# Twelve pipelined units in the preparation of the recurrence, and the condition vectors loaded first

## The chip, the cores and the metric

The kernel runs on one core of a Trainium2 chip, in one launch. The metric is the device time of that launch in microseconds (us), as a median of runs. The core has five engines, each with an instruction queue of its own: TensorE (PE) multiplies matrices and writes to PSUM, VectorE (DVE), ScalarE (ACT) and GpSimd (POOL) work element by element, and SyncE (SP) here only issues DMA transfers between DRAM and SBUF. Queues run in order and meet through semaphores.

## The reference

Two transformer blocks follow one another on 1024 tokens of width 1024. The change touches the first block's token mixing, and there the RWKV branch (8 heads of 64), and the conditioning vectors ahead of it. Cut to what matters (`rw` is the convolved part of `h @ w_in` for the 1024 latent tokens, `rwc` that for the 256 context tokens):

```python
rw = depthwise_conv(u[..., RET_COLS:], conv_w)          # width 3, along the tokens

def rwkv_prepare(u, w0, w2, a0, a2, g2, k_k, k_a, r_k):
    r, k, v, wl_f, wl_b, al, gl_f, gl_b = split_cols(u, RWKV_SPLITS)
    def decay(wl, w0_d, w2_d):
        w_log = -jax.nn.softplus(-(w0_d + jnp.tanh(wl) @ w2_d)) - 0.5
        return heads(jnp.exp(-jnp.exp(w_log)))
    iclr = jax.nn.sigmoid(a0 + al @ a2)
    kk = heads(k * k_k)
    kk = kk / jnp.maximum(jnp.linalg.norm(kk, axis=-1, keepdims=True), 1e-12)
    k_mod = heads(k * (1.0 + (iclr - 1.0) * k_a))
    bonus = (jnp.sum(r * k_mod * r_k, axis=-1, keepdims=True) * v)
    g_f, g_b = jax.nn.sigmoid(gl_f) @ g2[0], jax.nn.sigmoid(gl_b) @ g2[1]
    return (r, decay(wl_f, ...), decay(wl_b, ...), k_mod, v, -kk, kk * heads(iclr), g_f, g_b, bonus)
# the recurrence then runs forward and backward over these, in chunks of 64 tokens
```

At the very start, `silu(c) @ w_mod + b_mod` and `silu(c_ctx) @ w_mod + b_mod` give shifts, scales and gates (`w_mod` is 1024 x 6144, 25.2 MB in f32).

## The kernel before

The program is a chain of stages. A stage (`Stage`) allocates its tiles and semaphores, runs blocks in which each engine has its own code, and ends with a meeting of all engines and the clearing of its semaphores; the next stage starts after that. Nothing of a stage overlaps the next. The stages around the change are, in order: a block that loads two tables (`cst`, `col`); `modulation` (tiles `mod_*`); the norms and projection (`norm_*`, `proj_*`, which writes `uT`, the projected channels as rows over 1280 tokens); `retention` (`ret_*`); `rwkv_prepare` (`prep_*`); `rwkv_chunks` (`chunks_*`), which turns each of 40 blocks of 128 tokens by 128 channels into small matrices; `rwkv_states` (`states_*`), which runs the recurrence over 20 chunks from them; `rwkv_combine` (`comb_*`).

`modulation`: SP streams `w_mod` as 24 transfers of 1 MB through a ring of six buffers; a buffer is taken again when PE has used it. PE cannot begin before ACT has applied silu to the two vectors. ACT issues the two vector loads with one value (4 bytes) a descriptor, then 40 small loads of bias and gains, and only then waits for the vectors and applies silu.

`rwkv_prepare` has two blocks. The first convolves the four low-rank inputs on DVE. The second loops over `PAIRS` = 4 pairs of heads (128 channels, all `TT` = 1280 tokens at once). For one pair, DVE convolves r, k and v (L784 to L788, five instructions each), makes running sums of the decay rates (L980 to L986), normalises `kk` (L992 to L994, with a reciprocal of 1280 columns), and multiplies results out; POOL makes four of the eight results (L900). ACT applies Sigmoid, Square, Sqrt and Exp. The eight results of a pair go to DRAM (`prim`) through four buffers `prep_out`; v goes to `vT`; gates and bonus to `gate` and `bonus`. SP also stores the decay at each chunk's end, one value of 4 bytes at a time, to `wc` (L865), ahead of the eight stores of `prim` (L871) in its queue. All of a pair's products, stores and vector work use the same single buffers, and the next pair starts when DVE has seen all of it done (L1013 to L1015).

`rwkv_chunks` loads for each block `prim` (L1069), `vT` (L1070) and `wc` (L1072); PE waits for all three. `rwkv_states` loads all of `wc` (L1480) ahead of `re` in SP's queue (16 transfers, tile `states_r`), and ACT's queue loads `yi` beside it; DVE's first step waits for `wc`, PE's fourth for the first eight transfers of `re`.

## Time and profile before

| | before |
|---|---|
| median of 3 runs | 5389.64 us (5381.85 to 5392.05) |
| the profiled execution, its own time | 5381.96 us |
| its span, first to last instruction | 5379.8 us |
| mean granted clock of TensorE | 0.886 of full speed (2.4 GHz) |
| PE busy | 4132.7 us, 77% of the span |
| DVE busy | 2557.6 us, 48% |
| ACT busy | 1687.2 us, 31% |
| POOL busy | 409.5 us, 8% |
| DRAM traffic | 844.30 MB, mean 157 GB/s |

These shares are means over stages that have different limits. Since stages don't overlap, each is to be read by itself: its length, and what its engines wait for. On this core a product of f32 matrices stands in the trace as two records; the number behind `x` of a PE row counts records.

### The profile page before, as it was taken

To read this page: it belongs to the slowest core of one execution; us is meant where nothing else is said; L and a number is where in the kernel's file an instruction comes from. 1 tells how busy PE (TensorE), PEld (TensorE's weight loads), DVE (VectorE), ACT (ScalarE), POOL (GpSimd) and SP (SyncE) were. 2 spreads that over 40 slices of the span, in tenths; PEclk is the share of its full clock that TensorE was granted. 3 is DMA by queue.
4 is the path that set the end of the run, shared out by engine and by line. 5 is a ranking of instruction groups with operands and counts; after the bars stand their busy time and mean duration, and the time that the engine had idled before them with its cause. 6 is when DMAs were issued, how large, how long until landed. Compare 5 with 4: busy or idle time off the path is not lost. (4 is left out here: it accounts for less than half of the span.)

```text
span 5379.8 us, 73242 instructions
## 1 busy us (share of the span) xinstructions
PE 4132.7 (77%) x29105; PEld 2868.8 (53%) x29105; DVE 2557.6 (48%) x3932; ACT 1687.2 (31%) x3120; POOL 409.5 (8%) x317
## 2 busy tenths in 40 slices
PE   3799954124888572999957999696779887499995
PEld 1688844013888431676636644385644444266663
DVE  2311157675666436665633265424630134366664
ACT  1211022232555311444422144313630022144442
POOL 0000011011000300000000032000000000100001
PEclk7899977566999786999978999898989988699998
DMA  6222111486332332999962322122112221499997
GB/s 232 76 88 80 67 68 47 78 134 132 80 80 76 122 121 87 371 368 365 364 229 91 126 99 71 68 90 91 46 57 70 82 67 69 172 373 384 383 383 288
DMA packets 454569, 844.30 MB, mean 157 GB/s; under 512 B 77552, under 2 KB 277328, under 8 KB 451080
## 3 DMA queue, kind: packets, MB, share of 16 engines
q1 hardware_dynamic: 435448, 785.58, 42.6%
q0 software_dynamic: 12032, 41.96, 2.5%
q10 hardware_dynamic: 6800, 12.71, 0.7%
q8 instruction: 205, 3.36, 0.3%
q14 instruction: 84, 0.69, 0.0%
HBM read 675.72 MB, written 164.45 MB: 156 GB/s over the span
## 5 line engine op out<-in xcount | busy, mean ns | idle before, releaser
L395 PE MATMUL psum<-proj_hi,proj_w 128*128 128x512 f32 (+2 forms) x1728 | 461.2, 356 | 34.9 <-DVE proj_lo L461 34.9
L395 PEld LDWEIGHTS psum<-proj_hi,proj_w 128*128 128x128 f32 (+1 forms) x1728 | 305.4, 189 | 82.7 <-issue 35.1
L2380 PE MATMUL psum<-qkv_w,hT 128*128 128x512 f32 x768 | 334.6, 595 | 12.6 <-DMA qkv_w<-in_w_in 12.6
L2172 ACT ACTIVATE moe_hi<-moe_raw 128x2048 fp32r<-128x2048 f32 x128 | 245.1, 1917 | 301.2 <-PE psum L2123 248.2
L2207 DVE TENSOR_TENSOR moe_lo<-moe_raw,moe_hi 128x2048 fp32r<-128x2048 f32 x128 | 291.7, 2289 | 87.8 <-ACT moe_hi L2172 85.8
L395 PE MATMUL psum<-proj_lo,proj_w 128*128 128x512 f32 (+2 forms) x864 | 306.8, 355 | 0.0
L3748 DVE TENSOR_TENSOR moe_lo<-moe_raw,moe_hi 128x2048 fp32r<-128x2048 f32 x128 | 287.1, 2285 | 33.9 <-ACT moe_hi L3714 33.8
L3714 ACT ACTIVATE moe_hi<-moe_raw 128x2048 fp32r<-128x2048 f32 x128 | 238.5, 1906 | 28.5 <-DMA moe_raw<-in_w_gate_up 28.5
L2380 PEld LDWEIGHTS psum<-qkv_w,hT 128*128 128x128 f32 x768 | 145.4, 191 | 189.1 <-issue 175.9
L2968 PE MATMUL psum<-branches_T,mixed_w 128*128 128x512 f32 x512 | 222.0, 597 | 14.1 <-DMA mixed_w<-in_w_attn_o 14.1
L2133 PE MATMUL psum<-moe_wd,moe_hidT 128*128 128x512 f32 x512 | 225.0, 598 | 8.2 <-DVE moe_hidT L2228 8.2
L412 DVE COPY proj_out<-psum 128x512 f32<-128x512 f32 (+3 forms) x54 | 32.5, 602 | 412.9 <-PE psum L395 412.9
L3680 PE MATMUL psum<-moe_wd,moe_hidT 128*128 128x512 f32 x512 | 225.0, 592 | 0.9 <-DVE moe_hidT L3767 0.9
L395 PE MATMUL psum<-proj_g_hi,proj_g_w 128*128 128x512 f32 x512 | 159.8, 394 | 47.6 <-DVE proj_g_lo L461 47.6
L3672 PE MATMUL psum<-moe_hi,moe_xh 128*128 128x512 f32 x512 | 178.3, 429 | 9.8 <-DVE moe_lo L3748 9.8
L395 PE MATMUL psum<-proj_lru_hi,proj_lru_w 128*128 128x512 f32 x512 | 159.3, 392 | 31.9 <-DVE proj_lru_lo L461 31.9
L1407 DVE COPY_PREDICATED chunks_X<-chunks_msk,psum 128x128 f32<-128x128 int32 x400 | 107.6, 301 | 148.1 <-PE psum L1160 134.8
L395 PEld LDWEIGHTS psum<-proj_lo,proj_w 128*128 128x128 f32 (+1 forms) x864 | 162.7, 188 | 23.8
L2123 PE MATMUL psum<-moe_hi,moe_xh 128*128 128x512 f32 x512 | 168.0, 410 | 5.1 <-DVE moe_lo L2207 4.9
L2968 PEld LDWEIGHTS psum<-branches_T,mixed_w 128*128 128x128 f32 x512 | 98.2, 192 | 137.4 <-issue 137.4
L1320 ACT ACTIVATE chunks_T<-psum 128x128 f32<-128x128 f32 x400 | 102.9, 277 | 200.7 <-PE psum L1150 195.7
L2133 PEld LDWEIGHTS psum<-moe_wd,moe_hidT 128*128 128x128 f32 x512 | 98.1, 192 | 126.2 <-issue 116.2
(599 smaller groups left out, 8613.2 us busy)
## 6 DMA issues: line engine op xcount, KB each, us to landing
moe_raw<-in_w_gate_up SPq DMA_DIRECT2D x128, 1024.0 KB, 16.9
moe_raw<-in_w_gate SPq DMA_DIRECT2D x64, 1024.0 KB, 7.2
moe_raw<-in_w_up SPq DMA_DIRECT2D x64, 1024.0 KB, 7.4
moe_wd<-in_w_down SPq DMA_DIRECT2D x64, 1024.0 KB, 9.6
moe_wd<-in_w_down SPq DMA_DIRECT2D x32, 2048.0 KB, 11.7
mod_w<-in_w_mod SPq DMA_DIRECT2D x24, 1024.0 KB, 13.1
uT<-proj_out SPq DMA_DIRECT2D x35, 640.0 KB, 2.9
prim<-prep_out SPq DMA_DIRECT2D x32, 640.0 KB, 6.3
```

What stands on the lines that cost most here:

```text
L395: last = nc.tensor.matmul(bank[e * nch + c][0:width[e], 0:n], l, r, start=(k == 0 and i == 0), stop=(k == KD - 1 and i == 2))
L1407: nc.vector.copy_predicated(X[:, j, g, :, c], msk[:, g, 1 + l, :, c], Lb[g][:, P:3 * P].rearrange("p (h t) -> p h t", h=2)[:, :, c])\
L2123: last = nc.tensor.matmul(out[c][:, :], x[:, e % 2, k, :], w[:, n % R, i, c * BANK:(c + 1) * BANK], start=(k == 0 and x is xh and w is hi) ...
L2133: last = nc.tensor.matmul(y_bank[c][:, :], hidT[:, k, :], wd[:, j, i, c * BANK:(c + 1) * BANK], start=(k == 0), stop=(k == KD - 1))
L2172: nc.scalar.activation(hi[:, n % R], raw[:, n % R], ACT.Copy).then_inc(s["hi_ready"], 1)
L2207: nc.vector.tensor_tensor(lo[:, n % R], raw[:, n % R], hi[:, n % R], ALU.subtract).then_inc(s["lo_ready"], 1)
L2380: last = nc.tensor.matmul(bank[2 * (n % 2) + c_][:, :], hT[:, k, i * P:(i + 1) * P], w[:, m % 2, k, c_ * BANK:(c_ + 1) * BANK], start=(k = ...
L2968: last = nc.tensor.matmul(o[b][:, :], w[:, c // 2, n, k, (c % 2) * P:(c % 2 + 1) * P], act_T[:, n, k, b * BANK:(b + 1) * BANK], start=(k = ...
L3672: last = nc.tensor.matmul(out[:, :], x[:, e % 2, k, :], w[:, j, i, c * BANK:(c + 1) * BANK], start=(k == 0 and x is xh and w is hi), stop= ...
L3680: last = nc.tensor.matmul(y_bank[c][:, :], hidT[:, k, :], wd[:, e % RD, k, c * BANK:(c + 1) * BANK], start=(k == 0), stop=(k == 3))
L3714: nc.scalar.activation(hi[:, n % GU], raw[:, n % R], ACT.Copy).then_inc(s["hi_ready"], 1)
L3748: nc.vector.tensor_tensor(lo[:, n % GU], raw[:, n % R], hi[:, n % GU], ALU.subtract).then_inc(s["lo_ready"], 1)
```

## The change

Three things are changed. In words, with the names of the diff:

1. **Modulation.** The table block is gone; `cst` and `col` are loaded in the modulation stage from ACT's queue. The two vectors come from the host as one array `cvec`, 16 adjacent values a partition, in one transfer, and silu stands ahead of the 40 small loads.
2. **Preparation.** One block. The four pairs by three token ranges (256 context tokens, then 512 and 512) make twelve units. Unit `n` is convolved, put through the low-rank products and activations at step `n`, and finished at step `n+3`: at one step the engines work on a unit's front half and on an older unit's back half. The convolutions of r, k, v are nine products with diagonal matrices `dg` (made by POOL), added up in PSUM. Sigmoids are `(1+tanh(x/2))/2`, so that ACT needs one table for tanh and exp. The squared norms of a pair are gathered by products with `zsel` into 32 rows of 128 (`rs`), where root and reciprocal are taken once a pair, and spread again by products with `spread`. Results are multiplied in place, both directions in one DVE instruction; POOL makes no results, only the diagonals and the decays at chunk ends, which stay in SBUF (`wcol`).
3. **Later stages.** `rwkv_chunks` and `rwkv_states` read `wcol`; the loads of `wc` are gone.

The order of the instructions, as built. ACT's queue at the start of the program, before:

```order
L147 DMA mod_cc<-in_c 128x8x1
L148 DMA mod_cc<-in_c_ctx 128x8x1
L153 DMA mod_bias<-in_b_mod 1x512 x2
...
L156 DMA mod_g<-in_norm_gains 1x512
L159 ACT_TABLE_LOAD
L159 ACTIVATE mod_sc<-mod_cc 128x16
L169 DMA mod<-mod_m 1x512 x4
```

and with the change:

```order
L147 DMA mod_cc<-in_cvec 128x16
L149 DMA cst<-in_cst 128x880
L149 DMA col<-in_cols 128x171
L151 ACT_TABLE_LOAD
L151 ACTIVATE mod_sc<-mod_cc 128x16
L156 DMA mod_bias<-in_b_mod 1x512 x2
```

The silu has moved ahead of the 40 small loads, and two table loads have come ahead of it. Next PE in the preparation: the whole loop body before (one pair),

```order
L913 MATMUL psum<-prep_wl,prep_w2t 128x512 x2
L913 MATMUL psum<-prep_wl,prep_w2t 128x256
...
L913 MATMUL psum<-prep_al,prep_a2t 128x512
L913 MATMUL psum<-prep_al,prep_a2t 128x256
...
L918 MATMUL psum<-prep_prod,cst 128x512 x2
L918 MATMUL psum<-prep_prod,cst 128x256
L922 MATMUL psum<-prep_gl,prep_g2t 128x512 x4
L927 MATMUL psum<-prep_prod,cst 128x512 x2
```

and two steps with the change, one of a context unit (256 columns) and one of a latent unit (512), the back half's products first and last, the front half's between:

```order
L952 MATMUL psum<-prep_rs,prep_spread 128x128 x2
L912 MATMUL psum<-prep_rin,prep_dg 128x256 x9
L926 MATMUL psum<-prep_wl,prep_w2t 128x256 x2
L928 MATMUL psum<-prep_al,prep_a2t 128x256
L939 MATMUL psum<-prep_sqk,prep_zsel 32x128 x2
L952 MATMUL psum<-prep_rs,prep_spread 128x128 x4
L912 MATMUL psum<-prep_rin,prep_dg 128x512 x9
L926 MATMUL psum<-prep_wl,prep_w2t 128x512 x2
L928 MATMUL psum<-prep_al,prep_a2t 128x512
L939 MATMUL psum<-prep_sqk,prep_zsel 32x128 x4
L962 MATMUL psum<-prep_gl,prep_g2t 128x512 x2
L969 MATMUL psum<-prep_pb,cst 128x512
```

PE has taken over the convolutions, and has its spreading product at the head of each step. Last, DVE in a latent unit's back half:

```order
L1107 SCALAR_TENSOR_TENSOR prep_ex<-prep_keep,prep_th 128x512
L1108 SCALAR_TENSOR_TENSOR prep_xo<-prep_keep,prep_th 128x512
L1110 TENSOR_TENSOR prep_ex<-prep_ex,prep_th 128x512
L1113 TENSOR_TENSOR prep_ex<-prep_xo 128x512
L1115 TENSOR_TENSOR prep_ex<-prep_ex,prep_th 128x512
L1126 SCALAR_TENSOR_TENSOR prep_kk<-prep_u,prep_pcs,psum 128x512
L1128 TENSOR_TENSOR prep_u<-prep_u,prep_aff 128x512
L1130 SCALAR_TENSOR_TENSOR prep_th<-prep_th,prep_kk 128x512
L1135 SCALAR_TENSOR_TENSOR prep_pb<-prep_u,prep_pcs 128x512
L1146 SCALAR_TENSOR_TENSOR prep_ex<-prep_ex,prep_kk 128x1024
L1150 TENSOR_TENSOR prep_xo<-prep_ex,prep_th 128x1024
L1159 TENSOR_TENSOR prep_gt<-psum,prep_u 128x512
```

DVE's convolutions and its long reciprocal are gone from here, and the four products over both directions (two of them follow L1150 and are left out) have come in. The first instruction of a step is a running sum; the last waits for PE's last product of the step.

The diff, cut to the core:

```diff
 modulation, ACT:
-                    act.dma_start(cc[:, :, 0], c.rearrange("o (k p) -> p (o k)", p=P)).then_inc(c_in, 16)
-                    act.dma_start(cc[:, :, 1], c_ctx.rearrange("(k p) -> p k", p=P)).then_inc(c_in, 16)
+                act.dma_start(cc[:, :, :], cvec).then_inc(c_in, 16)
+                for dst, src in tables:
+                    act.dma_start(dst, src).then_inc(tables_in, 16)
+                act.wait_ge(c_in, 16)
+                nc.scalar.activation(sc[:, :, :], cc[:, :, :], ACT.Silu).then_inc(silu, 1)
...
 rwkv_prepare:
+    PARTS = [(0, TC), (TC, BANK), (TC + BANK, BANK)]
+    NP = len(PARTS)
+    UNITS = PAIRS * NP
+    STEPS = UNITS + NP
+        ring, st_bank, mid = [bank[0], bank[1], bank[7]], bank[5], bank[6]
 SP:
+                for n in range(STEPS):
+                    if n >= NP:
+                        store_unit(n - NP)
+                    if n < UNITS - NP:
+                        sp.wait_ge(s["ring_mm"], ring_at["r", n] + 1)
+                        load_unit(n + NP)
 PE:
+                def conv(n):
+                    ...
+                    for which in "kvr":
+                        o, k = place((which, n)), STREAM[which]
+                        for t in range(3):
+                            ins = nc.tensor.matmul(o[:, 0:m], dg[:, p % 2, 3 * k + t, :], rin[:, c, k, t:t + m], start=(t == 0), stop=(t == 2))
+                        ins.then_inc(s["ring_mm"], 1)
+                def widen(n):
+                    pe.wait_ge(s["rinv"], p + 1)
+                    if lat(n):
+                        pe.wait_ge(s["bonus"], lat(n))
+                    if n:
+                        pe.wait_ge(s["kk"], n)
+                    for j in range(a // P, (a + m) // P):
+                        ins = nc.tensor.matmul(mid[:, j * P - a:(j + 1) * P - a], spread[g:g + 32, j, :], rs[g:g + 32, :], start=True, stop=True)
+                    ins.then_inc(s["sp_mm"], 1)
+                for i in range(STEPS):
+                    n = i - NP
+                    if n >= 0:
+                        widen(n)
+                    if i < UNITS:
+                        conv(i)
+                        lora(i)
+                        select(i)
+                    if n >= 0 and latent(n):
+                        gates(n)
+                        summed(n)
 ACT:
+                for i in range(STEPS):
+                    n = i - NP
+                    if i % NP == 0 and n >= 0:
+                        roots(n // NP)
+                    if i < UNITS:
+                        conv_out(i, "k")
+                        conv_out(i, "v")
+                    if n >= 0:
+                        exponentials(n)
+                    if i < UNITS:
+                        conv_out(i, "r")
+                        tanhs(i)
+                    ...
+                    if 0 <= n + 1 < UNITS:
+                        affine(n + 1)
+                    if n >= 0 and latent(n):
+                        gate_out(n)
 DVE:
+                def rates(n):
+                    dve.wait_ge(s["twice"], n + 1)
+                    if n >= 2:
+                        dve.wait_ge(p_out[n % 2], 16 * 8 * (n // 2))
+                    f = link(nc.vector.tensor_tensor_scan(e[:, 0, 0, 0:m], keep[:, 0:m], t[:, 0, 0:m], 0.0, ALU.mult, ALU.add))
+                    ...
+                def keys(n):
+                    if c == 0:
+                        dve.wait_ge(s["root"], p + 1)
+                        wait(link(nc.vector.tensor_scalar(rs[g:g + 32, :], rs[g:g + 32, :], 1e-12, 2.0, ALU.max, ALU.mult)))
+                        nc.vector.reciprocal(rs[g:g + 32, :], rs[g:g + 32, :]).then_inc(s["rinv"], 1)
+                    dve.wait_ge(s["sp_mm"], n + 1)
+                    ...
+                def results(n):
+                    dve.wait_ge(s["exps"], 3 * n + 1)
+                    ...
+                    if latent(n):
+                        dve.wait_ge(s["bon_mm"], lat(n + 1))
+                        nc.vector.tensor_tensor(gt[:, 2, 0:m], mid[:, 0:m], un[:, 2, 0:m], ALU.mult).then_inc(s["bonus"], 1)
+                for n in range(UNITS):
+                    rates(n)
+                    keys(n)
+                    results(n)
...
 rwkv_chunks, SP:
-                        sp.dma_start(wct[:, j], wc[ds(q, 1)].rearrange("o d c n -> c (o d) n")).then_inc(s_in[j], 16)
 rwkv_states:
-                    for d in range(2):
-                        sp.dma_start(w[:, d], wc[:, d].rearrange("q c n -> c q n")).then_inc(w_in, 16)
-                dve.wait_ge(w_in, 32)
```

With the change, SP's queue in the preparation holds 173 transfers: 1 table, 48 loads (four a unit), 12 stores of `vT`, 96 of `prim` (eight a unit, 128 or 256 KB each), 8 of `gate` and 8 of `bonus`.

## Rows read from the trace of the kernel before

**Rows 1.** Windows: busy PE, PEld, DVE, ACT, POOL (records), granted clock, DMA share, GB/s.

```profile
640.00:972.00 332.00, 170.01 (x982) 139.00 (x981) 195.61 (x337) 87.86 (x195) 41.45 (x19) 0.76 0.15 51
1079.00:1148.00 69.00, 19.29 (x36) 8.74 (x36) 52.08 (x34) 20.44 (x23) 12.93 (x5) 0.60 0.84 140
1298.00:1768.00 470.00, 404.56 (x13080) 384.67 (x13080) 284.69 (x1120) 231.50 (x1000) 41.46 (x40) 0.97 0.31 81
```

**Rows 2.** Timeline, modulation: start, length, idle before and its releaser.

```profile
4.53 34.10 SPq L141 DMA_DIRECT2D mod_w<-in_w_mod  x13
30.20 0.22 ACT L159 ACTIVATE mod_sc<-mod_cc 128x16 f32<-128x16 f32 x1
81.54 1.89 PE L181 MATMUL psum<-mod_w,mod_sc 128*2 128x512 f32 x8 [0.56 <-DMA mod_w<-in_w_mod]
92.97 0.39 SPq L232 DMA_DIRECT2D norm_c_gs<-mod  x1
```

**Rows 3.** View by windows, of the modulation.

```profile
50.00:60.00 10.00, 6.43 (x28) 0.43 (x32) 0.00 (x0) 0.00 (x0) 0.00 (x0) 0.53 1.02 425
```

**Rows 4.** Waits, preparation's loop: total us, times, longest.

```profile
POOL prep_out L900 <- DMA prim<-prep_out: 73.1, 8, 18.8
```

**Rows 5.** Timeline of the preparation: one pair, its end, and the next stage.

```profile
982.04 0.89 DVE L784 TENSOR_SCALAR prep_wl<-prep_raw,col 128x1280 f32<-128x1280 f32 x1 [7.47 <-DMA prep_ex<-uT]
1060.48 19.20 SPq L871 DMA_DIRECT2D prim<-prep_out  x8
...
1289.54 1.14 SPq L877 DMA_DIRECT2D gate<-prep_gt  x1
1298.48 0.36 SPq L1065 DMA_DIRECT2D chunks_msk<-in_msk  x1
1308.24 1.98 PE L1132 MATMUL psum<-chunks_pr 64*64 64x128 f32 x32 [39.69 <-DMA chunks_wct<-wc]
```

**Rows 6.** Groups by line and form, preparation's loop: busy us, mean ns.

```profile
L993 DVE RECIPROCAL prep_prod<-prep_prod 128x1280 f32<-128x1280 f32 x4 | 32.6, 8152 | 0.1
L994 DVE TENSOR_TENSOR prep_kk<-prep_kk,prep_prod 128x1280 f32<-128x1280 f32 x4 | 13.6, 3411 | 0.1
L1003 DVE SCALAR_TENSOR_TENSOR prep_out<-prep_kk,prep_ex 128x1280 f32<-128x1280 f32 x8 | 11.6, 1488 | 0.6
L981 DVE TENSOR_TENSOR_SCAN prep_raw<-prep_keep,prep_sig 128x1280 f32<-128x1280 f32 x4 | 11.3, 2824 | 0.1
L955 ACT ACTIVATE prep_ex<-prep_cum 128x2560 f32<-128x2560 f32 x4 | 9.3, 2336 | 0.0
L955 ACT ACT_TABLE_LOAD x4 | 5.1, 1283 | 0.1
```

**Rows 7.** PE's weight loads in one pair: their starts space the records.

```profile
1032.14 0.34 PEld L918 LDWEIGHTS psum<-prep_prod,cst 128*128 128x128 f32 x1 [0.52 <-issue]
1032.99 0.34 PEld L918 LDWEIGHTS psum<-prep_prod,cst 128*128 128x128 f32 x1 [0.52 <-issue]
1035.01 0.19 PEld L922 LDWEIGHTS psum<-prep_gl,prep_g2t 128*128 128x128 f32 x1 [0.24 <-issue]
1035.44 0.19 PEld L922 LDWEIGHTS psum<-prep_gl,prep_g2t 128*128 128x128 f32 x1 [0.24 <-issue]
```

**Rows 8.** PE alone in a window behind that pair: busy, clock, DMA.

```profile
1040.00:1042.00 2.00, 0.00 (x0) 0.60 0.23 54
```

**Rows 9.** DMA issues in the loop (KB, median us to landing); a later timeline row.

```profile
wc<-prep_ex SPq DMA_DIRECT2D x16, 5.0 KB, 14.3
1303.55 2.81 SPq L1070 DMA_DIRECT2D chunks_vt<-vT  x1
```

**Rows 10.** Timeline of the states stage.

```profile
1768.83 8.02 SPq L1480 DMA_DIRECT2D states_w<-wc  x2
1788.63 1.63 DVE L1530 SCALAR_TENSOR_TENSOR states_S<-psum,states_w,nn 128x64 f32<-128x64 f32 x8 [25.44 <-DMA states_w<-wc]
1796.62 0.51 PE L1515 MATMUL psum<-states_r,states_S 64*64 64x64 f32 x10 [1.80 <-DMA states_r<-re]
```

More of the change, by code:

```diff
@@ L775, in rwkv_prepare @@
[L775 to L789 removed]
+        rin = st.sb("rin", [P, NP, 3, BANK + 2])
@@ new lines, in rwkv_prepare @@
+        pcs, pch = st.sb("pcs", [P, PAIRS, PW]), st.sb("pch", [P, PAIRS, 5])
+        w2t, a2t, g2t = st.sb("w2t", [P, RW]), st.sb("a2t", [HD, RW]), st.sb("g2t", [P, 2, RW])
+        zsel, spread = st.sb("zsel", [P, 62]), st.sb("spread", [2 * 32, 10, P])
+        rs = st.sb("rs", [2 * 32, P])
+        names = ("tab_in", "pc_in", "w_in", "padded", "diag", "chain", "wl_conv", "al_conv", "gl_conv", "wl_tanh", "gl_tanh",
+                 "gl_gate", "halves", "ring_mm", "ring_ev", "z_mm", "tanh", "twice", "squared", "sel_mm", "root", "rinv",
+                 "cums", "exps", "aff", "km", "sp_mm", "kk", "b", "pb", "bon_mm", "bonus", "o0", "o1", "o2", "o3", "wc")
@@ new lines, in rwkv_prepare, with unit, blocks, latent @@
+        LORAS = ((wl, P, 0), (al, HD, 128), (gl[:, 0, :], P, 192), (gl[:, 1, :], P, 320))
+        def unit(n):
+            p, c = n // NP, n % NP
+            return p, c, PARTS[c][0], PARTS[c][1]
+        def blocks(n):
+            p, c, a, m = unit(n)
+            return slice(p * NBK + a // P, p * NBK + (a + m) // P)
+        def latent(n):
+            return n % NP > 0
+        def lat(n):
+            return sum(1 for t in range(n) if latent(t))
+        def pc(p, name, i=0):
+            return pcs[:, p, PCOL[name] + i:PCOL[name] + i + 1]
@@ L792, in rwkv_prepare @@
+        ring_at = {}
+        for n in range(STEPS):
+            for k in range(3 if n < UNITS else 0):
+                ring_at["kvr"[k], n] = len(ring_at)
+            for d in range(2 if n >= NP and latent(n - NP) else 0):
+                ring_at["fb"[d], n - NP] = len(ring_at)
+        STREAM = {"r": 0, "k": 1, "v": 2}
         with nc.Block() as block:
@@ L1477, in _ @@
             def _(sp):
-                with nc.allow_non_contiguous_dma("four values a channel"):
-                    for d in range(2):
-                        sp.dma_start(w[:, d], wc[:, d].rearrange("q c n -> c q n")).then_inc(w_in, 16)
                 loads(sp, r, re, r_in)
```

564 lines of the change are left out of this document (302 added, 262 removed).

## Prediction

> **What bounds the kernel now.** I read the table of the page first: PE is busy 77% of the span, so no engine sets the whole, and since no stage overlaps another, only the lengths of the four touched stages matter. The view by windows gives them. A pair of heads in the preparation takes about 69 us, in which PE works 19 us, DVE 52 and ACT 20, while the DMA share is 0.84 at only 140 GB/s [rows 1]. So a pair is a chain through all engines in turn, and no engine is its bound. The chain shows in the waits: POOL stands 73 us in eight waits for stores of `prep_out` [rows 4]. Those stores start 11 us after they could, because the four small stores of `wc` stand ahead of them: 5 KB each, 14.3 us to land [rows 9]. The whole stage runs from about 973 (the first DVE row at 982.04 stands behind 7.5 us of idling and two short fills) to 1298.48, where the next stage starts: 325.5 us [rows 5].
>
> In the modulation, silu stands at 30.20, though SP started the weights at 4.53; afterwards PE only follows the weights at 425 GB/s, and ends at 81.54 + 1.89 = 83.43 [rows 2, 3]. In the states stage DVE waits 25.4 us for `wc`, and PE's first use of `re` is at 1796.62, 27.8 us into the stage [rows 10]. The chunks stage in between is PE's own (405 of 470 us busy, [rows 1]) but for its start.
>
> **The modulation, term 1.** The weights are 25.2 MB; at 425 GB/s that is 59.2 us [rows 3]. With the table block gone SP starts at about 0.7 instead of 4.5, and silu at about 7 (a small transfer, 3 to 4 us, a table load of 1.28 as in [rows 6]), before the ring of six is full, so the stream never stops. Last transfer: 0.7 + 59.2 + some 2.2 for the first to begin and the last to land + 1.3 for the tables in between = 63.4; PE ends 2 later at 65.4. Behind PE nothing changes. **-18 us**. Bounds: if the ring's stop were all that goes, 3.8 + 7.5 = 11; at most 20.
>
> **The preparation, term 2.** First the prices. DVE on two operands: 1.49 us for 1280 columns [rows 6], which is one column in 1.04 ns and 0.16 fixed, so 1.22 for 1024, 0.69 for 512, 0.42 for 256. A running sum: 2.82 for 1280, so 1.22 for 512, 0.69 for 256. ACT: 2.34 for 2560 columns, which I split as 0.82 ns a column and 0.24 fixed: 1.08 for 1024, 0.66 for 512. The reciprocal, 8.15 for 1280, is 0.8 for 128. PE: a 512-column record starts every 0.43 us at the upper level of the clock and every 0.85 at the lower [rows 7], and a product is two records: 0.86 or 1.7; I take 128 columns as a quarter.
>
> Back half and front half of a 512-unit, one step:
> - DVE: 2 sums (2.44), 3 on two operands (2.07), 4 keys (2.76), 4 over both directions (4.88), the bonus (0.69), some 0.3 of dependent waits: 13.1 us.
> - ACT: Square and 3 copies (2.6), 3 tanh (2.0), 3 Exp and the +1 (4.3), affine and 2 gates (2.0): 10.9 us.
> - PE: 9 + 3 + 2 + 1 products of 512 (12.9) and 8 of 128 (1.7): 14.6 us.
> - SP: 15 issues, at 0.4 to 0.7 each some 8 us. DMA: 3.9 MB, which at 276 GB/s (eight stores of 655 KB in 19.2 us, waits included, [rows 5]) is 14 us.
>
> These run beside each other, so PE paces. One hand-over adds to it: the PSUM tile `mid` serves the spread norms and the bonus sum, so the spreading at the head of a step waits for DVE's bonus, which waits for PE's last product: 0.69 + two passages of 0.15 = 1.0 in which PE stands. I walked one such step through the queues: exponentials start when ACT has taken k and v out (about 6 us into the step), DVE's results end 12.5 us in, the bonus then waits 2 for PE. So 15.6; the two low-rank products on separate row halves may overlap (0.9), and I take **15**.
>
> A context unit (256 columns, no gates) costs PE 6.0. But its spreading needs the root of the pair: DVE's sums of the same step come first (3.0), then the clamp and reciprocal (1.2), so PE stands 4.3 us at its head. Behind such a stop the clock is low: while PE idled it went to 0.60 in the window from 1040 [rows 8], and after idling, records came at 0.85 until 1033 and at 0.43 from 1035 [rows 7]. I add 2 us: 12.2. POOL's diagonals fall there too; beside POOL, DVE's two-operand work took 3.41 instead of 1.49 [rows 6], at most 2 us on two pairs, hidden under PE's next 15. If it weren't: +4.
>
> Three units are then 12.2 + 15 + 15 = 42. The stage: start 973; the low-rank inputs land at about 982 as now [rows 5], and PE's first products with them; three steps of front halves only, the first at the low clock, 11 + 11.2 + 11.2 = 33.4, to 1015.4; the first root with its table load, 5; then 6 + 30 to 1056.4; two more triples to 1140.8; three back halves alone, paced by DVE, 9 + 13.5 + 13.3 to 1176.6; the last store's issue (1), from it to the next stage 7.8 (1290.7 to 1298.5, [rows 5]), and some 20 more semaphores to clear (1.5): 1187. **-111 us**. Bounds: without clock loss and with the overlap a triple is 39, -11 more, and with the fill shorter -15; with PE at the retention stage's clock, 0.76 [rows 1], +44 (below).
>
> On tables: a load took 1.283 us [rows 6]; before, 13 stood in the stage, after, 8, of which two (first root, last Exp) lie on the path. The Trainium skill, ScalarE: Activation LUTs, section Table sets: the hidden batching unit, puts tanh in the set of exp and a load at about 2.7 us. By that price the sum would be 2.8 us later; the trace has 1.283, and I keep it.
>
> **The later stages, terms 3 and 4.** PE's first product in the chunks stage waits for `wc`, 9.8 us in [rows 5]; behind `wc` the transfer of v lands little earlier, since masks of 1.6 MB share the DMA. **-1** (0 to -3). The states stage: `re` (4.2 MB) was issued from 1776.9 on, after 8.0 us of `wc` [rows 10]. Now it starts at once beside `yi`; its first half is in when 4.2 MB of both are, 12 us at 350 GB/s and 2.5 to land: 1783.3 for 1796.6, **-13**. The three steps ahead of it took 6.2 us (1788.63 to 1794.8) and would be done at 1778: so at best -18, at worst, if `yi` goes first, -7.
>
> **Sum**: 18 + 111 + 1 + 13 = 143. The profiled run took 5381.96, 7.7 below the median of the runs shown; I subtract from the median: 5389.6 - 143 = **5247 us**.
>
> **Rivals.**
> (a) *PE's clock does not hold.* Nine short products, then a wait for one of three PSUM banks, and a stop at every context unit. In the retention stage, 51% busy, the granted clock is 0.76; for it to be so here PE would have to be broken up likewise, where I count 84% busy, and the chunks stage at 86% has 0.97 [rows 1]. At 0.76, PE's 14.6 are 19.2: eight latent steps +4.6, four context ones +1.9: +44, 5291. At the lower level throughout: a step 30, a triple 79, the fill 57: the stage 345, and the whole 5378, which the start and the states still hold below 5390. Chance 0.17. By the Trainium skill, TensorE: Matmul & The Clock Gate, section A second HAM failure mode: psum-queue depth-cycling, matmuls that cycle through PSUM banks can idle between groups often enough that the clock swings between its levels. That rule is this rival's; what the rows bear out is only the swing after long idling.
> (b) *SP's queue becomes the bound, and the kernel slower.* 173 transfers stand in one queue, in order. Where the DMA was full, a plain load held the queue for 2.81 us [rows 9]; at that price it is 486 us, 160 more than the whole stage now, and 5389.6 + 160 - 32 = 5518. It decides from (325.5 + 32)/173 = 2.07 us an issue on. Against it: eight stores of 655 KB took 19.2 us with their waits, and pieces here are 128 or 256 KB. Chance 0.04.
> (c) *The stores hold the stage, as they hold POOL now.* All its traffic, 37.8 MB at 276 GB/s, is 137 us, less than the 214 I expect, so not by itself; but if each unit's stores end as a burst that `rates` two units on has to wait for, one landing a unit is added, most of those 7.8, say 6: +70, 5317. Chance 0.04.
>
> **How the numbers follow.** My forecast, PE as pace near the full clock, has 0.75, and 5222 to 5275 as its own range (the bounds of the terms: -15, -5, -2 and +4, +6, +7, and a step 1 us off, 8). The range over all, **5222 to 5315**, takes in (a) down to 0.76 and all but (c)'s middle; outside are (b), the low end of the clock and surprises. A measurement of this kernel tells about 0.2%, 11 us: faster 0.93, same 0.03, slower 0.04 ((b), and (a) at its worst between same and faster).
>
> **What would show it.** Right: silu at about 7 and PE's end in the modulation at 65; PE busy above 80% from the fourth unit on, at a clock of 0.9 or more; latent steps 15 us apart, with PE waiting about 1 us for the bonus; a stop of 4 us at each context unit, ended by the reciprocal; the stage about 214 us; the states' first use of `re` about 14 us in. Wrong: latent steps 18 us apart or more; weight loads of `dg` spaced at 0.85; waits of `rates` for the stores of two units back; ACT as the releaser of PE's ring, which would mean that ACT, not PE, paces.

## The result, and the profile after

| | before | after |
|---|---|---|
| median | 5390.85 us (4 runs, 5381.85 to 5400.74) | 5254.65 us (4 runs, 5247.26 to 5272.68) |
| ratio | | 0.9751, 95% interval 0.9732 to 0.9771 |
| profiled execution, its span | 5381.96, 5379.8 us | 5261.83, 5259.5 us |
| mean granted clock of TensorE | 0.886 | 0.903 |

The forecast was 5247 us, range 5222 to 5315, faster with a chance of 0.93. Stage by stage, in the two profiled executions:

| part | forecast | measured |
|---|---|---|
| modulation: start of the next stage | -18 | 92.97 -> 79.25: -13.7 |
| preparation | 325.5 -> 214: -111 | 325.5 -> 219.9: -105.6 |
| chunks | -1 | 470.35 -> 471.7: +1.4 (its first product 0.3 earlier, 9.45 us in) |
| states, until the next stage's first product | -13 | 65.3 -> 52.6: -12.7 |
| sum up to there | -143 | -130.4 (1834.13 -> 1703.69) |
| the rest of the program | 0 | +10.1 |

The modulation of the changed kernel, by its timeline (start, length, and in brackets the idle time before and its releaser) and by windows (busy PE, PEld, DVE, ACT, POOL, granted clock, DMA share, GB/s), answering to [rows 2, 3]:

```profile
5.86 0.21 ACT L151 ACTIVATE mod_sc<-mod_cc 128x16 f32<-128x16 f32 x1 [2.43 <-DMA mod_cc<-in_cvec]
68.62 1.04 PE L183 MATMUL psum<-mod_w,mod_sc 128*2 128x512 f32 x8 [0.69 <-DMA mod_w<-in_w_mod]
79.25 0.38 SPq L234 DMA_DIRECT2D norm_c_gs<-mod  x1
```

```profile
60.00:62.00 2.00, 0.79 (x4) 0.11 (x8) 0.00 (x0) 0.00 (x0) 0.00 (x0) 0.71 1.04 434
62.00:64.00 2.00, 1.39 (x12) 0.11 (x8) 0.00 (x0) 0.00 (x0) 0.00 (x0) 0.50 0.76 315
64.00:66.00 2.00, 1.59 (x8) 0.00 (x0) 0.00 (x0) 0.00 (x0) 0.00 (x0) 0.50 0.13 53
66.00:68.00 2.00, 1.77 (x8) 0.11 (x8) 0.00 (x0) 0.00 (x0) 0.00 (x0) 0.58 0.06 25
```

Silu stands at 5.86, a little ahead of the 7 that I expected, and the stream of weights never stops. But the DMA's full rate ends at about 63.5, and then one or two of the sixteen engines (a share of 0.06 to 0.13, 25 to 53 GB/s) go on until 68, with PE waiting for their parts of the last transfers.

The preparation (959.38 to 1179.31) by windows: the fill up to the first spreading, three triples of units, the drain; then the chunks stage. They answer to the second and third of [rows 1].

```profile
959.40:1008.10 48.70, 29.99 (x93) 15.79 (x93) 20.20 (x24) 18.55 (x29) 22.13 (x40) 0.78 0.56 153
1008.10:1051.50 43.40, 38.23 (x124) 20.27 (x124) 31.57 (x42) 26.91 (x43) 14.60 (x15) 0.93 0.66 191
1051.50:1095.30 43.80, 38.74 (x125) 20.63 (x125) 31.48 (x42) 26.91 (x43) 14.60 (x15) 0.93 0.75 215
1095.30:1139.40 44.10, 38.99 (x124) 20.82 (x124) 31.19 (x42) 29.41 (x47) 5.11 (x6) 0.92 0.65 188
1139.40:1179.30 39.90, 16.55 (x32) 7.81 (x32) 27.31 (x35) 9.92 (x13) 6.49 (x7) 0.54 0.66 194
1179.30:1651.05 471.75, 407.08 (x13080) 387.04 (x13080) 285.04 (x1120) 231.85 (x1000) 41.49 (x40) 0.97 0.29 80
```

PE is busy 88% of a triple at 0.92 to 0.93 of the full clock: it paces, as forecast. The timeline shows its waits:

```profile
962.08 13.21 POOL L865 TENSOR_SCALAR prep_dg<-cst,prep_pcs 128x128 f32<-128x128 f32 x10 [1.34 <-DMA prep_pcs<-in_pcols]
973.79 6.72 PE L912 MATMUL psum<-prep_rin,prep_dg 128*128 128x256 f32 x18 [39.19 <-POOL prep_dg L865]
1008.09 1.22 PE L952 MATMUL psum<-prep_rs,prep_spread 32*128 32x128 f32 x4 [4.32 <-DVE prep_rs L1124]
1016.86 1.15 PE L952 MATMUL psum<-prep_rs,prep_spread 32*128 32x128 f32 x8
1032.49 1.12 PE L952 MATMUL psum<-prep_rs,prep_spread 32*128 32x128 f32 x8 [0.88 <-issue]
1179.31 0.34 SPq L1220 DMA_DIRECT2D chunks_msk<-in_msk  x1
```

`L952` is the spreading that opens a step. From 1016.86 to 1032.49 a latent step takes 15.6 us and ends in the hand-over of `mid` (0.88). At 1008.09, and again at 1051.51, 1095.27 and 1139.42, PE has stood 4.2 to 4.3 us for the reciprocal. New against the forecast is the start: one diagonal on POOL takes 1.29 us in the median, TensorE's first product waits for nine of them, and it stands 14.4 us into the stage, not 9.

In the states stage, answering to [rows 10], `re` and `yi` start together, and the first use of `r` comes 14.3 us in (forecast: 14):

```profile
1651.05 8.79 SPq L1625 DMA_DIRECT2D states_r<-re  x16
1665.34 0.80 PE L1664 MATMUL psum<-states_r,states_S 64*64 64x64 f32 x10 [7.75 <-DMA states_r<-re]
1703.69 6.57 PE L1736 MATMUL psum<-y,comb_centre 128*128 128x512 f32 x8 [7.90 <-DMA comb_pcs<-in_pcols]
```

Of the 10.1 us given back later, 8.4 are in the attention stage, whose code is the same. Windows, before and after:

```profile
3664.00:3978.00 314.00, 218.93 (x1568) 171.11 (x1568) 190.05 (x374) 186.17 (x541) 0.32 (x3) 0.89 0.16 55
```

```profile
3534.60:3857.00 322.40, 228.33 (x1568) 178.47 (x1568) 190.05 (x374) 186.65 (x541) 0.32 (x3) 0.87 0.16 53
```

The same records, DVE busy for the same 190.05 us, and PE for 9.4 us more at a lower granted clock. In a second profiled execution of the changed kernel (below) the stage starts 130.0 us earlier than before and the span is 128.8 us shorter; there the attention stage takes 312.6 us:

```profile
3534.00:3846.50 312.50, 217.70 (x1568) 169.98 (x1568) 190.16 (x374) 186.32 (x541) 0.32 (x3) 0.89 0.16 55
```

So these 8 us belong to the one execution. In the twelve profiled executions of this document the stage took 312.6 to 314.3 us in six, 318.3 in one and 321.4 to 322.4 in five, whatever was changed ahead of it. One span alone therefore can't settle a difference under 10 us.

### The profile page after: what moved, and what is told of

The parts are those of the page before. It is cut to its first block and busy times, and to the rows that moved or that the text cites. A ratio compares the mean times of both kernels' runs of the same rounds, so it can differ in the third digit from the quotient of the medians.

```text
span 5259.5 us, 73582 instructions
## 1 busy us (share of the span) xinstructions
PE 4237.6 (81%) x29457; PEld 2929.0 (56%) x29457; DVE 2475.1 (47%) x3963; ACT 1713.8 (33%) x3199; POOL 420.4 (8%) x383
## 5 line engine op out<-in xcount | busy, mean ns | idle before, releaser
L2530 PE MATMUL psum<-qkv_w,hT 128*128 128x512 f32 x768 | 335.4, 595 | 13.1 <-DMA qkv_w<-in_w_in 13.1
L3118 PE MATMUL psum<-branches_T,mixed_w 128*128 128x512 f32 x512 | 222.5, 598 | 14.3 <-DMA mixed_w<-in_w_attn_o 14.3
```

Source lines behind the costliest of these rows:

```text
L2530: last = nc.tensor.matmul(bank[2 * (n % 2) + c_][:, :], hT[:, k, i * P:(i + 1) * P], w[:, m % 2, k, c_ * BANK:(c_ + 1) * BANK], start=(k = ...
L3118: last = nc.tensor.matmul(o[b][:, :], w[:, c // 2, n, k, (c % 2) * P:(c % 2 + 1) * P], act_T[:, n, k, b * BANK:(b + 1) * BANK], start=(k = ...
```

## Experiments

Stage lengths are from each kernel's profiled execution, ratios from its runs against those of the kernel before on the same chip.

**The modulation alone** (in the kernel before).

```diff
-    modulation(nc, bank, x["w_mod"], x["b_mod"], x["c"], x["c_ctx"], x["norm_gains"], mod)
+    modulation(nc, bank, x["w_mod"], x["b_mod"], tabs["cvec"], x["norm_gains"], mod,
+               [(cst[:, :], tabs["cst"]), (col[:, :], tabs["cols"])])
```

> The kernel before with the change of the modulation alone. Theory: the stages do not overlap, so it gains what the changed kernel gained there, 13.7 us (next stage at 79.3 instead of 93.0), 0.3% of 5390, whatever the preparation does. The 4 us that my forecast of 18 lacks are the last two transfers of the weights, which land 4 us after the DMA's full rate has ended. Rival 1: these 4 us are a chance of that one execution; then the next stage starts at about 75 here. Rival 2: part of the gain is given back in later stages that the DMA bounds; then the whole moves by under 8.

5383.2 us (7 runs) against 5403.5: 0.9959 (0.9944 to 0.9975). The next stage starts at 80.03, 12.9 earlier, and the last product again stands late:

```profile
68.55 1.89 PE L183 MATMUL psum<-mod_w,mod_sc 128*2 128x512 f32 x8 [1.42 <-DMA mod_w<-in_w_mod]
80.03 0.39 SPq L234 DMA_DIRECT2D norm_c_gs<-mod  x1
```

Rival 1 is out: 68.55 after 68.62 is no chance. The interval, 13 to 30 us, just holds the 13.7. In the profiled execution the gain was 12.9 at the next stage and 10.6 at the chunks stage; that stage then took 479.3 us for 470.4, and the attention stage 318.3 for 314.0, so that nothing of it was left in the span. That looks like rival 2, but the runs exclude it: at least 13 us were kept, and rival 2 asked for under 8. The two spans are an uneven pair. The profiled execution of the kernel before, 5381.96 us, is 9 below the median of its own series and 21.5 below the median of this one, while the profiled execution here, 5383.3, is at its kernel's median; and the DMA doesn't bound the chunks stage (share 0.3).

**The root earlier.** ACT's root of a pair goes from the head of the context step to behind the tanh of the step before, and DVE's clamp and reciprocal ahead of the previous unit's bonus.

```diff
-                    if i % NP == 0 and n >= 0:
-                        roots(n // NP)
...
                         tanhs(i)
+                        if i % NP == NP - 1:
+                            roots(i // NP)
...
+                    if n % NP == NP - 1 and p + 1 < PAIRS:
+                        norms(p + 1)
                     if latent(n):
                         dve.wait_ge(s["bon_mm"], lat(n + 1))
```

> The changed kernel, with the root of a pair's sums moved to the end of ACT's previous step and the clamp and reciprocal on DVE ahead of the previous unit's bonus. Theory: TensorE's stop of 4.3 us at the three context units goes, and with it the low clock behind it (2.4 us each); stage 219.9 - 3 x 6.7 = 200, the kernel 5235. Rival 1: the clock stays low in the context unit for another reason; stage 207, 5242. Rival 2: the stop only moves, since DVE now waits for the root ahead of the bonus and TensorE for the bonus; stage 215 or more, 5250.

5247.35 us against 5403.5: 0.9712 (0.9698 to 0.9726); the stage 209.3, 10.6 shorter. Between the theory (200) and rival 2 (215). The first stop, at the end of the fill, is still 3.8 us, the second 2.0 and the third 1.8. Behind the second the 256-column convolution took 5.8 us, so the lower clock was still there for most of it; behind the third it took 4.15, its length at the full clock:

```profile
1050.01 0.68 PE L952 MATMUL psum<-prep_rs,prep_spread 32*128 32x128 f32 x4 [2.01 <-DVE prep_rs L1137]
1050.61 5.84 PE L912 MATMUL psum<-prep_rin,prep_dg 128*128 128x256 f32 x18
1090.13 0.68 PE L952 MATMUL psum<-prep_rs,prep_spread 32*128 32x128 f32 x4 [1.83 <-DVE prep_rs L1137]
1090.74 4.15 PE L912 MATMUL psum<-prep_rin,prep_dg 128*128 128x256 f32 x18
```

ACT's table load for the root came only behind the tanh and the +1. So the stop's cause was right and the cure too weak; the next version of it is below. The ratio is 21 us lower than the changed kernel's 0.9751, though the stage gave only 10.6 and the chunks stage was 8.7 us longer here (480.4). In the series of the modulation alone, on the same chip, the ratio also gave more than the stage (22 us for 12.9). The kernel before took 5403.5 us on that chip, 13 to 17 more than in its other series, and what lies behind that stays open: the ratios of that chip are not to be held against those of others within 10 us.

**The first pair's diagonals on DVE.**

```diff
-                diagonals(0)
+                pool.wait_ge(s["diag"], 9)
                 diagonals(1)
...
+                        nc.vector.tensor_scalar(dg[:, 0, 3 * k + t, :], ident, pc(0, nm, t), None, ALU.mult).then_inc(s["diag"], 1)
```

> The changed kernel, with the first pair's nine diagonals on DVE instead of POOL. Theory: TensorE's first product at 14.4 us into the stage waits for nine products on POOL of 1.16 us each; on DVE they take some 0.2 to 0.3 each, and the first product stands at about 8 us. The first low-rank product then waits for DVE's convolution and tanh, so the fill starts 5 us earlier in effect: stage 215, kernel 5250. Rival: the fill is paced by the low-rank inputs and ACT, and the diagonals were not on the path: stage 220, no gain.

5266.1 us against 5403.5: 0.9746 (0.9728 to 0.9763), no different from the changed kernel's 0.9751; the stage 224.1. Timeline:

```profile
963.43 1.85 DVE L1164 TENSOR_SCALAR prep_dg<-cst,prep_pcs 128x128 f32<-128x128 f32 x9 [5.24 <-DMA prep_pcs<-in_pcols]
968.39 6.70 PE L912 MATMUL psum<-prep_rin,prep_dg 128*128 128x256 f32 x18 [32.45 <-DMA prep_rin<-uT]
976.37 2.66 ACTq L998 DMA_DIRECT2D prep_g2t<-in_rwkv_g  x4
979.13 1.27 ACT L1060 ACTIVATE prep_wl<-prep_wl 128x1282 f32<-128x1282 f32 x1 [37.21 <-issue]
980.51 1.22 PE L926 MATMUL psum<-prep_wl,prep_w2t 64*128 64x256 f32 x4 [5.43 <-DMA prep_g2t<-in_rwkv_g]
```

Nine diagonals take 1.85 us on DVE, and the first product comes 7.7 us into the stage. Yet the first low-rank product stands at 980.51, 19.8 in, where it was 21.1 in: ACT, in order, waits for the low-rank weights and issues four more transfers ahead of its first tanh. The rival held, with another culprit than it named. The stage is even 4.2 us longer than in the changed kernel: the convolution of the second unit takes 9.8 us for 8.0, so the first spreading stands 50.6 us in for 48.7, and the second triple takes 46.1 us for 43.8, since one of its latent convolutions takes 9.7.

**The states' factors back through DRAM** (one part of the change undone).

```diff
+                        sp.dma_start(w[:, d], wc[:, d].rearrange("q c n -> c q n")).then_inc(w_in, 16)
                 loads(sp, r, re, r_in)
...
+                dve.wait_ge(w_in, 32)
+                        act.dma_start(wc[:, d].rearrange("q c n -> c q n"),
+                                      wcol[:, d, :].rearrange("p (q n) -> p q n", n=2)).then_inc(s["wc_out"], 16)
```

> The changed kernel, with one part undone: the factors of the states stage go to DRAM again (two transfers at the start of the chunks stage) and are loaded at the head of the states stage, ahead of re. Theory: the states stage is 12.7 us longer, as before, because re starts 8 us later and the first step waits for 5 KB in pieces of four or eight bytes; the chunks stage unchanged; kernel 5267. Rival 1: re is held up by yi on the other queue and not by these loads; then 0 to 4 us. Rival 2: the two stores delay the first products of the chunks stage, and it is longer by up to 14 us too.

5302.9 us against 5403.5: 0.981 (0.9795 to 0.9825). The states stage is 59.1 us long for 47.1, +12.0, with the first factor 19.8 us in, just as before:

```profile
1710.73 1.43 DVE L1690 SCALAR_TENSOR_TENSOR states_S<-psum,states_w,nn 128x64 f32<-128x64 f32 x7 [25.78 <-DMA states_w<-wc]
```

So term 4 is shown. But rival 2 holds besides, and worse: the chunks stage is 511.5 us for 471.7. Its start in this kernel, and in the changed one:

```profile
1179.00:1220.00 41.00, 12.57 (x234) 10.47 (x235) 7.12 (x24) 4.34 (x18) 4.03 (x4) 0.62 1.18 103
1204.10 1.98 PE L1286 MATMUL psum<-chunks_pr 64*64 64x128 f32 x32 [38.72 <-DMA chunks_vt<-vT]
```

```profile
1179.00:1220.00 41.00, 29.48 (x770) 27.28 (x772) 18.01 (x69) 13.63 (x57) 6.12 (x6) 0.77 0.38 111
```

Two stores of 40 KB each, in pieces of 8 bytes, fill the DMA engines (share 1.18 at 103 GB/s), hold ACT's queue for 28 us, and put off the first product by 15 us. The other 25 us are lost soon after: from 1220 to 1300 PE makes 1876 records for 2296, from 1300 to 1400 2839 for 2970, and then the two kernels keep pace. By the Trainium skill, DMA: Bandwidth & Descriptors, section Specifications, transfers want 512 bytes or more for full rate; the rows agree.

**The bonus sum in the ring.** `mid` then serves the spreading alone.

```diff
-                    nc.tensor.matmul(mid[:, 0:m], pairx, pb[:, 0:m], start=True, stop=True).then_inc(s["bon_mm"], 1)
+                    nc.tensor.matmul(place(("s", n))[:, 0:m], pairx, pb[:, 0:m], start=True, stop=True)\
+                        .then_inc(s["ring_mm"], 1)
```

> The changed kernel, with the bonus sum in a tile of the ring of three instead of the tile that the spread norms use. Theory: TensorE then no longer stands at the head of a step until DVE has read the bonus (1.8 us in the steps of the third part, 0.1 in those of the second), nor at the drain; the stage is 4 x 1.8 = 7 us shorter, 213, the kernel 0.13% below the changed one. Rival 1: the ring has one more user a step, and TensorE waits there instead for ACT or DVE to empty a tile: stage 220. Rival 2: where TensorE no longer waits, DVE's 13.1 us of work and its waits become the pace: under 3 us.

5255.9 us against 5390.4: 0.9756 (0.9738 to 0.9773); the stage 215.4, 4.5 shorter. PE passes from the bonus to the next spreading without a gap:

```profile
1073.42 1.02 PE L971 MATMUL psum<-prep_pb,cst 128*128 128x512 f32 x2
1074.37 1.15 PE L955 MATMUL psum<-prep_rs,prep_spread 32*128 32x128 f32 x8
```

The hand-over costs 0.9 us where it occurs: this latent step is 14.7 us long for 15.6. In the loop it occurs three times, 2.6 of the 4.5 us. Of the others, 1.1 is the context unit's convolution in the second triple (5.4 us for 6.5), 0.4 the drain and 0.2 the fill. At the drain TensorE's wait of 3.5 us for the bonus went as well, and nearly nothing came of it, since PE's other waits there, of 3.9 and 4.8 us, end with DVE. My expectation had taken DVE's wait of 1.8 us, which holds the product's own duration too, for PE's.

**The fill.** Diagonals on DVE, ACT's queue in a new order; and, in the modulation, 24 loads of single bias rows merged into 8 of three rows.

```diff
                     if i == 0:
                         act.wait_ge(s["gl_conv"], 2)
                         nc.scalar.activation(gl[:, :, :], gl[:, :, :], ACT.Tanh, scale=0.5).then_inc(s["gl_tanh"], 1)
+                        act.wait_ge(s["w_in"], 32)
+                        for d in range(2):
+                            for h in range(2):
+                                act.dma_start(g2t[:, d, :].rearrange("c (p x) -> c p x", x=P)[:, :, HD * h:HD * h + HD],
...
+                        act.dma_start(bias[32 * j + r:32 * j + r + 1, :, :],
+                                      b_mod[0:1, :].rearrange("o (s c b) -> o s c b", c=COLT, b=BANK)[:, :, j, :]).then_inc(b_in, 16)
```

> The changed kernel, with the first nine diagonals on DVE, and on ACT's queue the two low-rank weights issued first and the four pieces of the gate weights issued only behind the first unit's tanh. In the run with the diagonals alone TensorE's first product came 6 us earlier, but its first low-rank product still stood 19.8 us into the stage, behind ACT, which waited for the weights and issued four transfers until 18.4 us in. Theory: that wait was the bound of the fill; the first low-rank product now stands at about 15 us, and the stage is 5 us shorter, 215. Rival: the low clock of TensorE at the start takes the gain back (its products of the second unit took 9.8 us for 8.0 when they came earlier); stage 220 or more. The modulation in the same kernel has its 24 loads of single bias rows merged into 8 of three rows. Theory: the engine that carries single rows ends last, and the last product of the modulation, at 68.6, comes 1 to 3 us earlier. Rival: it doesn't move.

5259.4 us against 5390.4: 0.9767 (0.9749 to 0.9785); the stage 220.8. The rival was right:

```profile
964.73 6.66 PE L912 MATMUL psum<-prep_rin,prep_dg 128*128 128x256 f32 x18 [32.51 <-DMA prep_rin<-uT]
973.37 0.70 PE L926 MATMUL psum<-prep_wl,prep_w2t 64*128 64x256 f32 x4 [1.98 <-DVE prep_al L1097]
976.35 0.74 PE L939 MATMUL psum<-prep_sqk,prep_zsel 128*32 128x128 f32 x4 [1.88 <-DMA prep_spread<-in_spread]
977.02 9.50 PE L912 MATMUL psum<-prep_rin,prep_dg 128*128 128x512 f32 x18
```

The first low-rank product comes 4.7 us earlier in the stage (16.4 in for 21.1), but between short waits for DVE and a table PE is at the lower clock for longer (9.50 us for 7.99), and the first spreading stands 47.6 us in for 48.7: 1.1 left of 6.7. And the stage is not shorter but 0.9 longer, for its second triple takes 46.1 us instead of 43.8, as with the diagonals alone. The hand-over of the bonus is 1.20 us there, and behind it the clock falls (granted clock 0.66 from 1075 to 1080):

```profile
1074.03 1.12 PE L952 MATMUL psum<-prep_rs,prep_spread 32*128 32x128 f32 x8 [1.20 <-issue]
1075.08 9.69 PE L912 MATMUL psum<-prep_rin,prep_dg 128*128 128x512 f32 x18
```

In the modulation the last product stands at 67.55, 1.1 earlier, and at 67.52 in the next kernel that has the merging; in the eight executions without it, it stands between 68.26 and 68.69. By the Trainium skill, DMA: Bandwidth & Descriptors, section Why a DMA increments its semaphore by 16 and not by 1, a transfer is spread over as many engines, up to 16, as divide its outer dimension on both sides, and on this path over the lowest-numbered ones: three rows go on three. For a single row that nothing splits I take it to mean one engine. That would be a straggler as the windows show it; the merging moved the end by only 0.7 to 1.2 of its 4 us, and the 16 single rows of gains are still there. The mechanism fits, and is not shown.

**The root earlier still.** The sums of squares ahead of the low-rank products, the root ahead of the tanh, clamp and reciprocal ahead of DVE's last product of the unit before.

```diff
-                        lora(i)
                         select(i)
+                        lora(i)
...
                         conv_out(i, "r")
+                        if i % NP == NP - 1:
+                            roots(i // NP)
                         tanhs(i)
...
+                        norms(p + 1)
                     dve.wait_ge(s["exps"], 3 * n + 3)
```

> The changed kernel, with the sums of squares ahead of the low-rank products on TensorE, the root ahead of the tanh on ACT, and clamp and reciprocal ahead of DVE's last product of the unit before. In the first version of this, TensorE's stop at a context unit shrank from 4.3 to 2.0 us, ended by the reciprocal, and the products behind it still ran at the lower clock. Theory: now the stop is gone but for the hand-over of the bonus, TensorE's clock holds there, a triple takes 38.5 instead of 43.8, and the stage is 203 (the step down of the clock is what a stop of 2 us costs). Rival 1: the clock in the context unit stays low without the stop; triple 41. Rival 2: ACT's table loads, now between the copies and the tanh, delay the ring, and TensorE waits for ACT; stage 210 or more.

5242.2 us against 5390.4: 0.9723 (0.9706 to 0.974); the stage 198.3, 21.7 shorter. Windows of its three triples, and the head of the second:

```profile
1003.10:1040.60 37.50, 35.80 (x125) 18.53 (x125) 31.70 (x43) 28.17 (x46) 14.60 (x15) 1.00 0.69 198
1040.60:1078.00 37.40, 35.77 (x124) 18.46 (x125) 31.48 (x43) 27.09 (x44) 14.31 (x15) 1.00 0.87 253
1078.00:1115.50 37.50, 35.81 (x125) 18.57 (x125) 31.26 (x43) 27.18 (x44) 4.20 (x6) 1.00 0.76 222
```

```profile
1040.60 0.68 PE L952 MATMUL psum<-prep_rs,prep_spread 32*128 32x128 f32 x4 [0.83 <-issue]
1041.20 4.15 PE L912 MATMUL psum<-prep_rin,prep_dg 128*128 128x256 f32 x18
```

A triple takes 37.5 us for 43.8 on average, PE is busy 95% of it at the full clock, and the context unit's convolution takes 4.15 us for 6.1 to 6.9. That is 3 times 6.3 us, 3.9 in the fill, and the drain 1.2 longer: 21.6. ACT's table loads, eight in the stage as before, cost nothing in their new place between the copies and the tanh. Rivals 1 and 2 are out. By the ratios the kernel gained 15 us on the changed one, each with an interval of 9 or more to either side, which doesn't tell it from the stage's 21.7; in its profiled execution the chunks stage is 478 us long, 6.3 more.

**All together**: the edits of the last one, the ring, the diagonals, the queue and the bias rows, as above.

> The changed kernel with all of this together: root, clamp and reciprocal early, the bonus in the ring, the first diagonals on DVE, ACT's queue in the new order, the bias rows merged. Theory: the parts add, since each takes away another of TensorE's waits: stage 220 - 17 - 7 - 5 = 191, kernel 5225 to 5230 where the changed kernel has 5255. Rival: DVE becomes the pace as soon as TensorE's waits are gone (13.1 us of work a step and its waits for the exponentials): stage 200.

5239.7 us against 5390.4: 0.9727 (0.9705 to 0.9749), the same as the last one; the stage 197.5. The rival has the size, though not the cause. With the bonus in the ring, PE's wait reappears there, behind ACT's gates and not behind DVE, in two of the three context units. The clock holds behind it all the same: these convolutions take 4.12 us.

```profile
1078.02 2.18 PE L917 MATMUL psum<-prep_rin,prep_dg 128*128 128x256 f32 x9 [1.87 <-ACT prep_gt L1057]
```

**The kernel before with its small stores behind the large ones.**

```diff
-                    for d in range(2):
-                        at = CH - 1 if d == 0 else 0
...
                     for n in range(8):
                         sp.wait_ge(s[f"out{n % 2}"], p * 4 + (n // 2 + 1))
...
+                    for d in range(2):
+                        at = CH - 1 if d == 0 else 0
...
```

> The kernel before, with the four small stores of wc behind the eight stores of prim instead of ahead of them. It asks how much of the preparation's 106 us came from taking these stores out of the way, which the change does along with the pipeline. Theory 1: POOL's 73 us and DVE's 48 us of waits for stores lie mostly in series with the rest of a pair, and the small stores delay the first of them by 11 us, so each of four pairs is 8 to 11 us shorter: 5390 - 40 = 5350. Theory 2: the chain of a pair goes through DVE, ACT and PE at other places, and the stores of a pair are then held by the small ones behind them, which ACT's exponentials of the next pair wait for; gain under 12 us.

5388.4 us against 5386.5: 1.0003 (0.9995 to 1.0012); the stage 328.0 us (971.73 to 1299.77), for 325.5, and for 327.6 in the kernel with the modulation alone: no shorter. Waits (total us, times, longest), and under them DVE's of the kernel before:

```profile
POOL prep_out L900 <- DMA prim<-prep_out: 50.1, 8, 10.8
ACT prep_gt L947 <- DMA gate<-prep_gt: 27.2, 3, 10.0
DVE prep_out L1005 <- DMA prim<-prep_out: 23.1, 8, 3.2
```

```profile
DVE prep_out L1005 <- DMA prim<-prep_out: 47.7, 8, 11.1
```

POOL's 73.1 us [rows 4] fell to 50.1 and DVE's 47.7 to 23.1, and nothing came of it: ACT now waits for the store of the gates, which stands behind the small ones. The time is theory 2's; that this one wait closes the chain is read from the table and not tested.

**The changed kernel again**, without an edit.

> The changed kernel once more, unchanged. The chunks stage, whose code and work are the same in all of these kernels but one, took 470, 472, 479, 480, 475, 477, 475, 478 and 475 us in nine executions. Theory: its length is a matter of the execution and not of the kernel ahead of it: here it may be anywhere from 470 to 480, while the modulation (79.2), the preparation (219.9) and the states (47.1) repeat within 1 us. Rival: each kernel has its own length there; then it is 472 again.

5260.9 us against 5386.5: 0.9768 (0.9753 to 0.9782), span 5251.0. Preparation 219.9, states 47.1, chunks 471.6. So the theory, a length that differs from execution to execution, is not borne out for the one kernel seen twice (471.7 and 471.6). The rival, a length for each kernel, fits, but isn't shown. The chips differ too: the lengths of 475.2 to 480.4 were all taken on two chips, and this one and the 472.0 of the experiment before on a third. Within either of the two the kernels differ by 2.9 to 5.0 us, so the chip is not the whole of it. No kernel is on record with profiles from two of the three.

## Why the prediction held, and where it was off

- **The time**: 5247 forecast, 5254.65 measured, and the mechanism, TensorE as the pace near the full clock with one stop a triple, is the one in the trace. The stages gave 130.4 of the 143; the two series of the changed kernel, 0.9751 and 0.9768, are 134 and 125 us of 5390.
- **Modulation, 18 forecast, 13.7 measured.** "The stream never stops" was right, and 59.2 us at 425 GB/s too: the full rate ends at 63.5. What failed is the last term, 2.2 us "for the first to begin and the last to land": one or two engines finish 4 us later. Its size repeats; its cause is only argued.
- **Preparation, 111 forecast, 105.6 measured**, by its own steps:
  - First product 9 us in: 14.4, for POOL's nine diagonals of the first pair, which stand in no term of the fill (only those of later pairs were weighed, and called hidden). It cost little. By the experiments on the start, ACT's wait for the low-rank weights and then the low clock hold the fill as much; first spreading 48.7 in, forecast 47.4.
  - Latent step 15: 15.6 where the hand-over stands (the walk through the queues was right and the 0.6 taken off it was not), 14.7 where the context unit's stop swallows it. The row halves of the low-rank products do overlap (three products in 1.9 us instead of 2.6), but eighteen records of a convolution take 7.93 us instead of 7.74, the short products 2.05 instead of 1.7, gates and bonus 0.3 more.
  - Context step 12.2, as 4.3 of stop, 6.0 of work and 2 of clock: 13.1 to 13.7, as 4.2 to 4.3, 6.3 (its length where nothing stops it) and 2.5 to 3.2. This term of the clock was the one mis-sized in the triple: 42 forecast, 43.4 to 44.1 measured.
  - Drain 35.8: 34.2 (1134.4 to 1168.6). Tail 10.3: 10.7.
- **Chunks and states**: -1 was +1.4, and -13 was -12.7; undoing the latter alone gave 12.0 back.
- **Rival (a), the clock.** Over a triple it fell to 0.92 or 0.93 only by the stops; without them it is 1.00. By the Trainium skill, TensorE: Matmul & The Clock Gate, section A second HAM failure mode: psum-queue depth-cycling, matmuls that cycle through PSUM banks can idle often enough for the clock to swing; in this ring of three banks with PE 95% busy it did not. The rival's price was read from a window that starts 35 us ahead of the retention stage: from 675 to 972 that stage is 47% busy at 0.74, not 51% at 0.76, and the rival would have cost a little more than 44 us.
- **Rivals (b), (c).** SP's queue and the stores held nobody for long: the DMA share is 0.65 to 0.75, and at most 0.87 when the triples were six microseconds shorter. (The eight stores by which the forecast priced its DMA, 5.24 MB in 19.2 us, give 273 GB/s and not 276; no term changes by it.)
- **Where the gain came from.** The small stores of `wc`, which I named among the signs of the old chain, were worth nothing by being moved. The rest of the 106 us I did not take apart further: that it comes from the pipeline is argued from the trace, where PE is busy 88% of a triple for 28% of a pair before, and no run has the one part without the others. The three kernels with the lowest ratios keep the pipeline and shorten or remove PE's stop at the context units: 0.9712, 0.9723 and 0.9727, whose intervals overlap, with stages of 209.3, 198.3 and 197.5 us.

## What to carry to other kernels

In a pipeline whose pace is TensorE, look for the one stop a period: here a small reciprocal behind a queue of other work cost 4.3 us and 2.5 to 3.2 more in clock, and having it ready in time gave 21.7 us in a stage of 220. A wait that is large in the table need not be in series: two waits of together 121 us lost 48 and the stage got no shorter; another wait, of 27 us, had come up right behind. To price a start, follow every in-order queue to its first use, with what it issues and waits for on the way, and not only the first operand to be late.

## What was unexpected of the hardware

- POOL takes 1.29 us (median of 36, from 0.59 to 2.39) for a 128x128 f32 matrix times one value a partition; DVE made nine of them in 1.85 us.
- The chunks stage, with the same instructions on the same data sizes, takes 470.4 and 472.0 us in the kernel before and its reordered version, 471.7 and 471.6 in two executions of the changed kernel, and 475.2 to 480.4 in seven others whose code ahead of it differs (one of these, the modulation alone, is otherwise the kernel before). PE is busy for 407.1 us in one of 471.7 and 408.7 in one of 478.0, so most of the difference is time in which it stands. It repeated in the one kernel that was profiled twice, where the attention stage differed by 9.8 us; whether the code ahead of it, the chip or something else sets it stays open. At up to 8.7 us it is large beside the 21.7 that the best experiment gained in its stage, and it is why a stage's gain should be read in the stage.
- What a stop of TensorE costs in clock does not follow from its length alone. Behind 4.2 to 4.3 us the context unit's convolution took 5.4 to 7.0 us, behind 2.0 us 5.8, behind 1.83, 1.87 and 0.83 us 4.1 to 4.2, its length at the full clock. Yet behind hand-overs of 1.09 and 1.20 us, in the two kernels with only the diagonals or the fill changed, a latent convolution took 9.7 us for 8.0. What PE had done before these stops differs, and which part of it matters was not tested.
